# Latent attention on one core: the key stage's last steps in another order, the query's turns in two banks, and the next tile's first query products in the first cycle

## The reference, cut to what matters

```python
def mla_mixer(h, hc, p, cos, sin, with_ctx_out):
    def kv_heads(kv_a, k_r, n):
        kv = (rms_norm(kv_a, p["kv_a_norm"]) @ p["w_kv_b"]).reshape(B, n, 16, 64 + 64)
        k_nope, v = jnp.split(kv, [64], axis=-1)
        return rms_norm(k_nope, p["k_nope_norm"]), rms_norm(k_r, p["k_rope_norm"]), v
    def q_heads(q_a, n):
        q = (rms_norm(q_a, p["q_a_norm"]) @ p["w_q_b"]).reshape(B, n, 16, 64 + 32)
        return jnp.split(rms_norm(q, p["q_norm"]), [64], axis=-1)
    ...
    # keys and values of context and sequence are concatenated; for each block of 128 queries:
    s = (einsum('bqhd,bkhd->bhqk', q_nope, k_nope)
         + einsum('bqhr,bkr->bhqk', q_rope, k_rope)) * (64 + 32) ** -0.5
    o = einsum('bhqk,bkhd->bqhd', softmax(s), v)
    y = (o * silu(g)) @ p["w_out"]
```

## Time and profile before

| what | value |
|---|---|
| time, median of 3 runs | 3579.1 us (3571.78 to 3582.05) |
| profiled execution, its time | 3582.95 us |
| profiled execution, its span | 3581.0 us |
| PE busy (matrix products and turns) | 3388.5 us, 95% of the span |
| DVE busy | 1684.6 us, 47% |
| ACT busy | 1103.0 us, 31% |
| POOL busy | 500.1 us, 14% |
| granted PE clock, mean of the span | 0.979 of full |

### The profile page before, as it was taken

The page is one execution under the profiler, slowest core; times in us unless marked ns, Lnnn a source line. Parts: engine busy times, 40 slices in busy tenths (PEclk is TensorE's granted clock), DMA queues, the critical chain, the costliest instruction groups (busy, mean ns, idle before and its releaser), DMA issues.

```text
span 3581.0 us, 55879 instructions
## 1 busy us (share of the span) xinstructions
PE 3388.5 (95%) x23625; PEld 1969.3 (55%) x23625; DVE 1684.6 (47%) x2746; ACT 1103.0 (31%) x1863; POOL 500.1 (14%) x479
## 2 busy tenths in 40 slices
PE   8999999998899989899999999988998999899999
PEld 4466655654333334445655556555555777467764
DVE  2555666634211138334544445443225666466642
ACT  1333343311111125333333333342213444234430
POOL 0222222311100014011011011001012000200000
PEclk9999999999999999999999999999998999999999
DMA  3022211213899899200000000030200000000001
GB/s 115 25 66 72 66 38 54 90 55 144 343 340 375 301 383 358 50 18 19 1 18 19 18 18 12 2 133 18 78 0 13 1 1 14 24 1 1 1 27 68
DMA packets 115390, 302.64 MB, mean 85 GB/s; under 512 B 13142, under 2 KB 55446, under 8 KB 101958
## 3 DMA queue, kind: packets, MB, share of 16 engines
q1 hardware_dynamic: 78470, 231.86, 17.9%
q10 hardware_dynamic: 29760, 42.05, 3.2%
q0 software_dynamic: 6912, 25.17, 1.9%
HBM read 345.67 MB, written 55.10 MB: 112 GB/s over the span
## 4 chain that ended last, share of the span: by engine, by line
PE 81%; DVE 9%; ACT 5%; DMA 2%; issue 2%; POOL 1%; SPq 1%; another core or an unknown queue 0%; POOLq 0%; DVEq 0%; ACTq 0%
PE ps L2896 12%; PE ps L452 9%; PE ps L1845 6%; PE ps L2313 4%; PE ps L2914 4%; PE ps L2284 4%; PE ps L2358 4%; PE ps L3633 4%; PE ps L3919 3%; PE ps L3292 3%; PE ps L1269 3%; ACT sb L2258 3%; PE ps L1865 3%; PE ps L3620 3%; DVE sb L2340 2%; PE ps L3569 2%
## 5 line engine op out<-in xcount | busy, mean ns | idle before, releaser
L2896 PE MATMUL ps<-sb 128*128 128x512 f32 x960 | 467.8, 607 | 19.6 <-ACT sb L2196 10.9
L2258 ACT ACTIVATE sb<-ps,sb 128x1280 f32<-128x1280 f32 (+1 forms) x288 | 353.5, 1232 | 311.7 <-DVE sb L2342 293.2
L452 PE MATMUL ps<-sb 128*128 128x512 f32 x704 | 347.2, 613 | 4.8 <-DMA sb<-in_w_in 3.3
L2313 PE MATMUL ps<-sb 128*64 128x128 f32 x5248 | 318.8, 276 | 3.3 <-DVE sb L2373 1.8
L2313 PEld LDWEIGHTS ps<-sb 128*64 128x64 f32 x5248 | 283.9, 137 | 51.3 <-issue 47.0
L2079 POOL TENSOR_TENSOR sb<-sb 128x1 f32<-128x1 f32 (+3 forms) x114 | 131.4, 1154 | 1036.1 <-DVE sb L2075 1036.0
L2237 DVE TENSOR_REDUCE sb<-ps 128x2 f32<-128x2560 f32 (+1 forms) x80 | 191.8, 2398 | 147.5 <-PE ps L2914 147.5
L2300 DVE COPY sb<-ps 128x512 f32<-128x512 f32 x192 | 131.9, 689 | 251.4 <-PE ps L2284 250.7
L2896 PEld LDWEIGHTS ps<-sb 128*128 128x128 f32 x960 | 164.6, 193 | 137.2 <-issue 110.6
L2292 ACT ACTIVATE sb<-ps 128x512 f32<-128x512 f32 x144 | 85.5, 597 | 494.4 <-PE ps L2284 494.4
L2284 PEld LDWEIGHTS ps<-sb 128*128 128x128 f32 x1344 | 149.6, 142 | 158.5 <-issue 66.2
(11 more groups left out here) (387 smaller groups left out, 4858.0 us busy)
## 6 DMA issues: line engine op xcount, KB each, us to landing
sb<-in_exp_gate SPq DMA_DIRECT2D x65, 1024.0 KB
sb<-in_exp_up SPq DMA_DIRECT2D x65, 1024.0 KB
sb<-in_exp_down SPq DMA_DIRECT2D x65, 1024.0 KB
sb<-in_l_w_mod ACTq DMA_DIRECT2D x12, 2048.0 KB, 17.7
d_ys<-sb ACTq DMA_DIRECT2D x32, 512.0 KB, 4.2
d_ys<-sb SPq DMA_DIRECT2D x64, 256.0 KB
sb<-d_x SPq DMA_DIRECT2D x32, 512.0 KB, 3.8
sb<-in_w_in SPq DMA_DIRECT2D x22, 512.0 KB, 4.8
```

Source lines behind the costliest of these rows:

```text
L452: ins = pe.e.matmul(k.bank(6 + half), wt[i % 2][:, kk, :], xT[:, kk, half_of(half)], start=kk == 0, stop=kk == 7)
L2258: act.e.activation(self.Pb[g % 2][:, self.cols(g, b)], self.k.ps[:, self.cols(g, b)], ACT.Exp, bias=self.mx[:, i:i + 1], scale=-1.0, accum ...
L2313: ins = k.pe.e.matmul(k.bank(7)[64 * b:64 * b + 64, o:o + 128], values(c, b), self.PT[:, nk * b + c, :], start=c == 0, stop=c == nk - 1, s ...
L2896: ins = pe.e.matmul(k.bank(5), lhs[:, kk, :], w[:, kk, 512 * half:512 * half + 512], start=kk == 0, stop=kk == 7)
```

## The change

The steps around the end of the key stage and in the first attention cycle are put into another order. In the key stage, four slots of `bg` follow each step in place of three, and in the second half the gate's last turn comes behind the query chain. After step 9, the query's first turn stands ahead of the turn of key tile 8, and its second turn between that and the scaling of key tile 9; the second turn goes to bank 6 (`query_bank`) for the first query tile. The wait `keys_end` keeps what the positional products need, and a new `keys_all`, ahead of the `nope` products, has the rest. In cycle 0 the next tile's first three query products stand ahead of the turns of the probabilities.

```diff
     def keys(hh):
-        bg = itertools.chain(last_gate(0) if hh else (), queries(hh, 0))
+        bg = itertools.chain(queries(hh, 0), last_gate(0) if hh else ())
         for c in range(NTT):
             yield ("key", hh, c)
...
-            for _ in range(3):
+            for _ in range(4):
                 yield from slots(bg)
         yield ("wk", 1) if hh == 0 else ("wo",)
+        yield from (s for s in bg if s)
+        yield from (("qturn", hh, 0, 0), ("qTe", hh, 0, 0))
         yield ("kturn", hh, NTT - 2)
+        yield from (("qturn", hh, 0, 1), ("qTe", hh, 0, 1))
         yield ("kscale", hh, NTT - 1)
         yield ("kTe", hh, NTT - 2)
-        yield from (s for s in bg if s)
-        yield from (("qturn", hh, 0, 0), ("qTe", hh, 0, 0), ("qturn", hh, 0, 1), ("qTe", hh, 0, 1))
...
         elif kind == "qturn":
             hh, n, half = x
+            b = query_bank(n, half)
             pe.wait_ge(*t["q", hh, n])
-            pe.wait_ge(*free[5])
+            pe.wait_ge(*free[b])
...
         elif kind == "keys_end":
-            for tok in (free[2], free[3], free[4], free[6], free[7], t["kR"], t["kN"], t["v"]):
+            for tok in (free[2], free[3], free[4], t["kR"]):
+                pe.wait_ge(*tok)
+        elif kind == "keys_all":
+            for tok in (free[6], free[7], t["kN"], t["v"]):
                 pe.wait_ge(*tok)
...
+    def query_bank(n, half):
+        return 6 if half and n == 0 else 5
...
                 yield ("rope", 0, ("A2", "B1", "B2", "B0"))
+                yield ("keys_all",)
                 yield ("nope", 0, ("B0", "B1", "B2", "A2"))
...
+            if g == 0:
+                yield from at[r, 1]
             yield from (("pturn", g, 0), ("pturn", g, 1))
-            yield from at.get((r, 1), ())
+            if g:
+                yield from at.get((r, 1), ())
             yield from (("pturn", g, 2), ("pturn", g, 3), ("pturn", g, 4))
```

More of the change, by code:

```diff
@@ L3574, in pe_program @@
             hh, n, half = x
+            b = query_bank(n, half)
             pe.wait_ge(*t["q", hh, n])
-            pe.wait_ge(*free[5])
+            pe.wait_ge(*free[b])
             for j in range(4):
-                ins = pe.e.transpose(k.bank(5)[:, 128 * j:128 * j + 128], m.qd[:, 512 * (1 - half) + 128 * j:512 * (1 - half) + 128 * j + 128], ident)
+                ins = pe.e.transpose(k.bank(b)[:, 128 * j:128 * j + 128], m.qd[:, 512 * (1 - half) + 128 * j:512 * (1 - half) + 128 * j + 128], ident)
             ins.then_inc(*turned.up())
@@ L3691, in act_turn_out @@
             act.wait_ge(*tok)
-        act.e.activation(qN, k.bank(5).rearrange("p (j t) -> p j t", j=4), ACT.Copy).then_inc(*evac_a.up())
-        t["qN", hh, n] = free[5] = evac_a.at
+        b = query_bank(n, half)
+        act.e.activation(qN, k.bank(b).rearrange("p (j t) -> p j t", j=4), ACT.Copy).then_inc(*evac_a.up())
+        t["qN", hh, n] = free[b] = evac_a.at
         t["qk"] = t["qturn"]
```

## The result

The changed kernel takes 3537.76 us (median of 4 runs, 3534.78 to 3540.74) against 3576.84 us (median of 4, 3571.78 to 3582.05): ratio 0.9891, 95% interval 0.9878 to 0.9905. That is 39.1 us, or 1.1%. The forecast was a gain of 39.3 us and a time of 3541, a value between 3539.8 and 3543.7, which that gain gives from the median of before then known (3579.1) and from the profiled execution's 3582.95.

The account below looks back on a forecast made before the run. The prediction took the key stage's two-tile chain and half-clock first scores as bounds; five terms a half summed to -19.0 and -20.3, together -39.3 us, giving 3541 us, range 3532 to 3553.

Parts of the forecast that it names:

- The two bounds: Key stage: a two-tile chain of 4.3 to 4.7 us a tile; first scores: PE at half clock.
- (a): Key stage, to the last key product's end: four slots and early query copies give -2.4 and -3.9 us by half.
- the upper bound: Key stage, step 3: the query's three scalings on DVE cost at most 0.63 us more on each alternating chain.
- (b): Last key product's end to first scores: only the store stays on the chain, -4.4 and -3.8 us by half.
- (c): Scores of cycle 0: at full clock they take 7.3 us, -7.8 and -7.9 us by half.
- (d): Scores to probability turns: six query product instructions of 2.57 us fill the 2.47 us wait, +0.1 us a half.
- (e): Probability turns to the second cycle's scores: 3.1 us remain, -4.5 and -4.8 us by half.
- The weighing of the clock: Key stage end: a 3.3 us stretch, against 6.15 us that held and 6.42 that fell, keeps the clock up.
- the chance of 0.75: Whole kernel: the chance given to the forecast itself, a gain of 39.3 us with the clock staying up.
- both falls stay: Rival: the clock falls over the first scores in both halves; -21.5 us in all, 3558 us, chance 0.08.
- about 25 of the 39 us: Both halves: the share of the forecast gain said to depend on the clock staying up.
- slower: Rival: half clock outlasts the query products, attention cycles cost about 9.5 us more each; 3596 us, chance 0.03.

Follow-up runs that it names:

- e2: Kernel before the change with only four slots a step and the gate's turn behind the query chain; 3574.93 us in one traced execution.
- e1: Kernel before the change with only the new order at the end of the key stage; median 3559.76 us against 3577.50, ratio 0.9954.
- e3: Changed kernel with both query turns back in bank 5 behind the scaling of tile 9; 3563.54 us in one traced execution.
- e5: Kernel before the change with three extra 512-column products, results overwritten, between the query's two turns; 3563.55 us in one traced execution.
- e6: Kernel before the change with 24 extra turns of query data, results overwritten, between the query's two turns; 3560.60 us in one traced execution.
- e4: Changed kernel with the next tile's query products behind the first two probability turns again; 3541.56 us in one traced execution.
- e7: Changed kernel with the query's second turn in bank 5 like the first; 3553.42 us in one traced execution.
- e12: The kernel of e7 run again, unchanged; median 3550.69 us over four executions, ratio 0.9941 to the kernel before the change.
- e8: Changed kernel with keys_end asking for everything again; 3543.15 us in one traced execution.
- e11: Changed kernel run again as it is; median 3538.37 us, ratio 0.9889 to the kernel before the change.
- e10: The kernel of e7 with one extra 512-column product, result overwritten, ahead of the query's second turn; 3532.46 us in one traced execution.

## Why the prediction was right

The mechanism held, step by step; that the clock held with it was partly luck. **The two bounds** were read rightly: the chain of two tiles in the key stage, and the half clock behind the wait for the query's store. e2 gives the first alone, e1 and e3 separate the order from the rest, and e5 and e6 show that the clock by itself is worth 4.5 to 8.6 us a stage.

**(a)** is 0.2 and 0.3 us smaller than forecast. In the first half step 3 cost what the upper bound said: the root of tile 3 took 2.29 us beside the three scalings of the query, as the root of another step had before. I had counted 0.2 of the possible 0.63 there. In that half key products two apart start 8.69 (2 to 4), 9.51 (3 to 5), 9.09 (4 to 6) and then 8.80 us apart, where I had said 8.7 to 8.8; no PE wait up to the last key product is over 0.67 us in either half.

**(b)** is right to 0.2 us in both halves: the store of the positional part behind the sum of tile 9, with no scaling ahead of it, was the last thing waited for.

**(c)** stood on the clock, and it held. It is 0.3 to 0.4 us smaller because halving the half-clock times undercounts: the first rope group took 1.13 us, not 1.0, and the nope groups 1.91 and 2.34.

**(d)** and **(e)** are right as sums. But the step behind them, that the early products only fill a wait of 2.47 us and take 2.57, was incomplete. Taking them back costs 7.8 us in the two halves (e4), not 3.2, because the clock then falls behind the scores. With them in place this does not show in the sum, so the term was right for the changed kernel and would have been wrong for the kernel without them: right here by luck, since the forecast had not asked what the clock does in that wait.

**The weighing of the clock** came out on the right side, for a reason that was only half right. I compared lengths: a stretch of 3.3 us is half of those that held or fell. e7 shows that 0.6 us more is enough to lose it; the margin was far smaller than the two rows suggested, so the right side was partly luck, and the chance of 0.75 was, if anything, high. The rival *both falls stay* took 21.5 us off before; the two stages of e7 and e12 are together 20.4 and 22.1 us under those of before. So its price was right. By that price the two falls cost 17.8 us, and the "about 25 of the 39 us" that I hung on the clock was too much: e7 lies 17.6 above the change, of which 1.2 is the later start. The 25 was all of (c) and (e), but by the rival's own working 0.7 us a half of (c), and 2.6 and 3.0 us of (d) and (e), come whether the clock falls or not. The rival *slower*, in which the products do not bring the clock back, found nothing for it: in every traced run with a fall over or behind the scores, it ended during those products.

What stays open: why the clock holds in the one order and falls in the other is shown only as a matter of how much PE does and how soon the scores start. The same work can go either way, as the wait of 2.21 us in the key stage and the wait of 2.47 us behind the scores did; why is not shown. e8's single fall was not repeated.

## What to carry to other kernels

When a wait ends and the work behind it runs at half the granted clock, price the wait with that work, not by its own length: here a stretch of 7 to 8 us with little work was followed by scores that took 7.5 us longer in each half than they do now. First shorten the thin stretch by putting the last needed store ahead of work that nobody waits for yet; if a wait remains, put work there that is needed anyway, such as the next tile's products. Then test the margin: make the stretch half a microsecond longer and see whether the clock still holds. And trace more than one execution, since the clock of one can differ from that of the next.

## What the runs showed of the hardware that was not expected

- Turns hold PE's clock at its upper level: 24 of them, 2.78 us, in a wait of 3.6 us kept 1.00 over the scores that followed in e6's first half, as three products did in e5's second; in the other half of each the clock fell before the scores ended (0.87), where without them it was 0.50 over all of them.
- A difference of 0.6 us in the start of the scores decided between 1.00 and 0.51 to 0.57 over the scores, in both halves, twice (e7 and e12 against the change and e11), and one product of 1.02 us undid it (e10, both halves).
- The scores do not bring the clock back though PE is 95% to 100% busy with them (15.30 us at 0.50 in the earlier trace rows, 14.47 us in e3); in both it came back during the six query products that followed.
- An idle PE of 2.47 us with only turns ahead of the products was followed by a fall in both halves of e4, but not in the second half of e1.
- The same wait of 2.21 us in the same key stage was followed by a short fall in e1 and e5 and by none in before and e6.
